# First expert pair's rows: one-hot as weights with x moving in 512 columns, instead of x as weights in 128

## The chip, the cores and the metric

The kernel runs on 1 core of one Trainium2 chip. The metric is device time in microseconds, the median of several runs of the whole program. TensorE works at 2.4 GHz when the granted clock is 1.00, and at 1.2 GHz when it is 0.50.

## The reference, cut to what matters

A block with two layers of mixer and mixture of experts is followed by a second block with attention; 256 tokens, width 1024, float32. The change lies in the expert part of each layer:

```python
g_logits = xt @ w_group            # 4 groups, top 1
e_logits = xt @ w_expert           # 8 experts a group, top 2
...
xi = x_pad[rows]                   # the tokens of one expert
h = jax.nn.silu(xi @ w1[e]) * (xi @ w3[e])
return (h @ w2[e]) * rw[:, None]
```

32 experts with w1 and w3 of 1024x256 and w2 of 256x1024: 3 MB an expert, 96 MB a layer.

## The kernel before, in words

The program is written per engine, with semaphores. A layer runs in this order: norm, mixer (`mix`, whose last steps are the output projection and the router's logits), routing, 16 pairs of experts.

**Weights.** SyncE's queue issues all weights (L583 for w1 and w3, L589 for w2) into a ring of six slots; each load waits until TensorE has freed its slot. During the routing the slots fill up with the first experts' weights.

**Routing.** VectorE picks group and experts for each tile of 128 tokens (`choose`, its last operation L2021 signals `picked`). TensorE counts the picks (L1345, into bank 7). VectorE forms the places (L2033), and from them `first_hot` (L2035), which says for each token whether it stands in a slot of expert 0 or 1; then `token_of`, `slot_of` and `lane_hot_bf` (L2046) for all experts. ScalarE copies the scaled logits out (L1840), which frees banks 4 and 5. TensorE opens the four sum banks with products of zeros (`zero_acc`, L968), and forms tables by slot (`by_slot`, L1354): once the token numbers (bf16), later the gates (fp32). From the token numbers VectorE makes the row numbers (L2074), with which GpSimd fetches the rows of the pairs from 1 on by an indirect DMA from a copy of x in HBM (L826).

**The first pair.** Its rows are not fetched, since they would come late. TensorE forms them with products: for each of the 8 blocks k of the width, and each of the 2 token tiles, x[:, t, block k] is the stationary operand and first_hot the moving one (L1365). The block k takes every eighth element of a row of x. The result, 128 columns for each k, stands turned (width on the partitions) in banks 4 and 6. ScalarE copies it with the gain of each row to `xg` (L1847), four copies a half. Between the halves TensorE forms the token table.

**Pairs.** `expert_pair`: up products (L922, 32 instructions a pair), transposes of the next pair's rows (L862, `gather`), hidden turned (L942), down products (L954), and the sums by token of the pair before (L873). The first pair also forms the gates by slot within its up products. The first slot is freed by the first product of the second half of the up products.

Of the kernel before, what the change touches and what calls it, by code (L numbers as in the profile page):

```python
# [18 lines left out]
ACT = mybir.ActivationFunctionType  # L19
AX = mybir.AxisListType  # L20

P = 128
SEQ = 256
NT = SEQ // P
D = 1024
KD = D // P
# [8 lines left out]
PAIRS = NE // 2  # L35
# [24 lines left out]
HALF = 512  # L60
# [129 lines left out]
def program(nc, io, out, mixer=True, second=True):  # L190
    with ExitStack() as ctx:
# [3 lines left out]
        def sem(name):  # L195
            return ctx.enter_context(nc.semaphore(name))

        bank = [ctx.enter_context(nc.psum_tensor(f"bank{b}", [P, HALF], F32)) for b in range(8)]
        ring = [sb(f"ring{s}", [P, SLOT]) for s in range(RING)]
        x = sb("x", [P, NT, D])  # L200
# [6 lines left out]
        ident, ones = const["ident"], const["ones"]  # L207
# [25 lines left out]
        stats = sb("stats", [P, 16])  # L233
# [24 lines left out]
        expin = nxt(NT, 8)  # L258
        expout = nxt(NT, 8)
# [11 lines left out]
        first_hot = xf[:, :, :, :].rearrange("p t k i -> p (t k i)")[:, 0:NT * P]\  # L271
            .rearrange("p (t e s) -> p t e s", t=NT, e=2)
        lane_hot_bf = nxt(NT * CELL).bitcast(BF16).rearrange("p (t i s) -> p t i s", t=NT, i=2)
        token_of = nxt(NT * NE).bitcast(BF16).rearrange("p (t i e) -> p t i e", t=NT, i=2)
# [8 lines left out]
        x_rows = nxt(2, D)  # L283
# [214 lines left out]
        xfT_ready = sem("xfT_ready")  # L498
        logits_done = sem("logits_done")
        exp_wanted = sem("exp_wanted")  # L500
        kept_or_exp = sem("kept_or_exp")
        picked = sem("picked")

        rows_stored = sem("rows_stored")
        rows_landed = [sem(f"rows_landed{b}") for b in range(2)]
        LAYER_ROWS = [16 * (PAIRS // 2 - 1), 16 * (PAIRS // 2)]
        counted = sem("counted")
        over_ready = sem("over_ready")
        acc_done = sem("acc_done")
        hots_ready = sem("hots_ready")  # L510
# [204 lines left out]
        def _(pool):  # L715
# [33 lines left out]
            for l in range(DEPTH):  # L749
                m = PER * l  # L750
                if mixer:
# [7 lines left out]
                    half = ROPE // 2  # L759
                    for a in range(2):  # L760
                        g1, g2 = [qk_gain[:, a, NOPE + half * i:NOPE + half * (i + 1)].unsqueeze(1)
                                  .broadcast_to([P, NT, half]) for i in range(2)]
                        for i, (trig, g) in enumerate(((0, g1), (1, g2), (1, g1), (0, g2))):
                            ins = pool.tensor_tensor(rope_table(a, i), cos_sin[:, trig, :, :], g, ALU.mult)
# [40 lines left out]
                plan = plans[l]  # L805

                copied(pool, plan, "yTa0", "yTa1")
                pool.memset(x_rows[:, 0, :], 0.0)
                pool.memset(y_words[:, 1, :], 0.0)
                step(pool.memset(onehot_words[:, 1, :], 0.0))  # L810
                copied(pool, plan, "out0", "out1")
# [45 lines left out]
        def _(pe):  # L857
# [107 lines left out]
            def zero_acc():  # L965

                for b in range(4):
                    pe.matmul(bank[b][:, :], zeros[:, 0:P], zeros, start=True, stop=False, skip_group_check=True)  # L968

            for s in range(RING):  # L970

# [363 lines left out]
            for l in range(DEPTH):  # L1335
                turn(l, range(1 if l == 0 else NT))
                mix(l)
                zero_acc()

                pe.wait_ge(picked, 2 * l + 2)  # L1340
                before, every = counts_bf[:, 0, :], counts_bf[:, 1, :]
                for at, parts in ((0, ((before, 0),)), (1, ((before, 1), (every, 0))), (2, ((every, 0), (every, 1)))):
                    terms = [(mask, t, i) for mask, t in parts for i in range(2)]
                    for n, (mask, t, i) in enumerate(terms):
                        ins = pe.matmul(bank[7][:, at * NE:(at + 1) * NE], mask, pick[:, t, i, :],  # L1345
                                        start=(n == 0), stop=(n == len(terms) - 1))
                ins.then_inc(counted, 1)

                def by_slot(dst, hot, values, kinds):

                    for e in range(2):
                        for t in range(NT):
                            for i in range(2):
                                ins = pe.matmul(dst[CELL * e:CELL * (e + 1), 0:kinds * PAIRS], hot[:, t, i, 0:CELL],  # L1354
                                                values(t, i, e),
                                                start=(t == 0 and i == 0), stop=(t == NT - 1 and i == 1))
                    ins.then_inc(tables_made, 1)

                q0 = l * PAIRS
                pe.wait_ge(kept_or_exp, 3 * l + 2)  # L1360
                pe.wait_ge(hots_ready, 2 * l + 1)
                for half in range(2):
                    for k in range(4):
                        for t in range(NT):
                            ins = pe.matmul(bank[4 + 2 * half][:, k * P:(k + 1) * P],  # L1365
                                            x[:, t, :].rearrange("p (i k) -> p k i", k=KD)[:, 4 * half + k, :],
                                            first_hot[:, t, :, :].rearrange("p e s -> p (e s)"),
                                            start=(t == 0), stop=(t == NT - 1))
                    ins.then_inc(main["gathered"], 1)
                    if half == 0:  # L1370
                        pe.wait_ge(hots_ready, 2 * l + 2)
                        by_slot(bank[7][:, P:P + PAIRS], lane_hot_bf,
                                lambda t, i, e: token_of[:, t, i, :].rearrange("p (q e) -> p e q", e=2)[:, e, :], 1)

                def gates_by_slot():

# [243 lines left out]
        def _(act):  # L1620
# [213 lines left out]
            for l in range(DEPTH):  # L1834
                if mixer:
                    norm_turn(l)
                    mix(l)
                for t in range(NT):
                    act.wait_ge(picked, 2 * l + t + 1)
                    act.activation(logits[:, t, :], bank[4 + t][:, 0:N_GROUPS + NE], ACT.Copy,  # L1840
                                   scale=stats[:, 8 + t:9 + t]).then_inc(kept_or_exp, 1)
                act.wait_ge(loaded_ffn, ROUTER_LOADS * (l + 1))
                for half in range(2):
                    act.wait_ge(main["gathered"], 2 * l * PAIRS + half + 1)
                    for i in range(4):
                        k = 4 * half + i
                        ins = act.activation(xg[:, 0, k, :], bank[4 + 2 * half][:, i * P:(i + 1) * P], ACT.Copy,  # L1847
                                             scale=row_gain_in[:, k:k + 1])
                    ins.then_inc(main["xg_ready"], 1)
                act.wait_ge(exp_wanted, l + 1)  # L1850
                act.activation(expout[:, :, 0:7], expin[:, :, 0:7], ACT.Exp).then_inc(kept_or_exp, 1)
                q0 = l * PAIRS
                act.wait_ge(gates_ready, 2 * l + 2)
                last = PAIRS // 2 - 1
                with act.Fori(0, last) as j:
                    for par in range(2):
                        expert_pair(par, 2 * j + (q0 + par), main)
                for par in range(2):
                    expert_pair(par, 2 * last + (q0 + par), main, last=(par == 1))
                act.wait_ge(over_ready, l + 1)  # L1860
                n_over = act.value_load(overint[0:1, l, CELLS_OVER:CELLS_OVER + 1], min_val=0, max_val=2)
                with act.If(n_over > 0):
                    S = extra[l]
                    act.wait_ge(extra_slots[l], OVER_PAIRS + 1)
                    with act.Fori(0, n_over) as j:
                        for par in range(2):
                            expert_pair(par, 2 * j + par, S)
                with act.Else():
                    act.nop()
# [80 lines left out]
        def _(dve):  # L1950
# [74 lines left out]
            def route(l):  # L2025
# [3 lines left out]
                choose(l, 1)  # L2029
                dve.wait_ge(picked, 2 * l + 2)  # L2030
                step(dve.tensor_tensor(first_place, pick[:, :, 0, 0:2], pick[:, :, 1, 0:2], ALU.add))
                dve.wait_ge(counted, l + 1)
                step(dve.scalar_tensor_tensor(first_place, bank[7][:, 0:NT * NE].rearrange("p (t e) -> p t e", t=NT)  # L2033
                                              [:, :, 0:2], 1.0, first_place, ALU.add, ALU.mult))
                dve.tensor_tensor(first_hot, const["iota"][:, 1:CELL + 1].unsqueeze(1).unsqueeze(1)  # L2035
# [10 lines left out]
                dve.tensor_tensor(lane_hot_bf, lanes, places, ALU.is_equal).then_inc(hots_ready, 1)  # L2046
                dve.tensor_tensor(lane_hot[:, :, :, 0:CELL], lanes, places, ALU.is_equal)

                dve.wait_ge(kept_or_exp, 3 * l + 2)
                gl, el = logits[:, :, 0:N_GROUPS], logits[:, :, N_GROUPS:]  # L2050
                gw = [groupwork[:, :, i, :] for i in range(3)]
                rb = lambda n: rowmax[:, :].unsqueeze(2).broadcast_to([P, NT, n])
# [28 lines left out]
            def finish_route(l):  # L2081


                dve.wait_ge(kept_or_exp, 3 * l + 3)
                step(dve.tensor_reduce(expin[:, :, 0:1], expout[:, :, 0:N_GROUPS], AX.X, ALU.add))
                step(dve.tensor_tensor(expin[:, :, 1:2], expout[:, :, 5:6], expout[:, :, 6:7], ALU.add))
                step(dve.tensor_tensor(expin[:, :, 0:1], expin[:, :, 0:1], expin[:, :, 1:2], ALU.mult))
                step(dve.reciprocal(expin[:, :, 0:1], expin[:, :, 0:1]))
                step(dve.tensor_tensor(expin[:, :, 0:1], expin[:, :, 0:1], expout[:, :, 4:5], ALU.mult))
                rstd = stats[:, 8:8 + NT]  # L2090
                step(dve.tensor_tensor(gates.rearrange("p i t -> p t i"), expin[:, :, 0:1].broadcast_to([P, NT, 2]),
                                       expout[:, :, 5:7], ALU.mult))
                step(dve.tensor_tensor(gates, gates, rstd.unsqueeze(1).broadcast_to([P, 2, NT]), ALU.mult))
                by_token = gates.rearrange("p i t -> p t i").unsqueeze(3).broadcast_to([P, NT, 2, NE])
                step(dve.tensor_tensor(gate_of[:, :, :, 0, :], pick, by_token, ALU.mult))
                dve.tensor_tensor(gate_of[:, :, :, 1, :], pick,
                                  rstd.unsqueeze(2).unsqueeze(3).broadcast_to([P, NT, 2, NE]), ALU.mult)\
                   .then_inc(gates_ready, 1)
# [605 lines left out]
```

## Time and profile before

| | us |
|---|---|
| median of 3 runs | 1101.12 |
| lowest, highest | 1099.44, 1103.45 |
| the profiled execution | 1100.17 |
| its span | 1098.3 |
| mean granted clock of TensorE | 0.992 |

A span runs from the first instruction to the last on the core; the time of the execution lies 1.87 us above it. An fp32 product is two matmul instructions, each with its weight load (PEld). "Idle before" a row is the time in which its engine waited, and behind the arrow stands what ended it.

### The profile page before, as it was taken

The numbers are of one execution on the slowest core, as the hardware profiler recorded it, in microseconds if no ns is written. First come the engines' busy times: TensorE is split into PE (matmuls) and PEld (weight loads), VectorE is DVE, ScalarE is ACT, GpSimd is POOL, SyncE is SP. The second block draws the span as 40 slices with busy tenths as digits, with TensorE's granted clock in tenths as the row PEclk, the third lists the DMA queues.
The fourth block names the chain that finished last, engine by engine and source line by source line (L and its number), as shares of the span: only waits on it lengthen the run. The fifth ranks groups of instructions, "written<-read, shape, count | busy, mean of one in ns | idle before, by whom it ended". The sixth has DMA issues, their size and how long they took to land.

```text
span 1098.3 us, 12899 instructions
## 1 busy us (share of the span) xinstructions
PE 1053.3 (96%) x4563; PEld 543.0 (49%) x4597; DVE 401.2 (37%) x975; ACT 272.8 (25%) x530; POOL 99.7 (9%) x146
## 2 busy tenths in 40 slices
PE   6999999999999999999989999999999999999998
PEld 3577655333333334676655333333334844555543
DVE  1164424443443351462343443344430222333221
ACT  4244322111111003334321111111112005564300
POOL 1220221000000002210121000000000200000000
PEclk9899999999999999999999999999999999999999
DMA  8526227999999996427246999999979537822000
GB/s 299 195 78 256 103 87 246 386 412 411 412 413 412 411 399 208 128 82 302 77 172 228 398 412 413 412 412 412 413 289 389 199 36 201 310 85 77 1 1 38
DMA packets 95326, 280.44 MB, mean 255 GB/s; under 512 B 15957, under 2 KB 29699, under 8 KB 86960
## 3 DMA queue, kind: packets, MB, share of 16 engines
q1 hardware_dynamic: 90208, 273.27, 65.9%
q0 software_dynamic: 5072, 6.56, 1.7%
q8 instruction: 29, 0.48, 0.2%
q14 instruction: 17, 0.14, 0.0%
HBM read 286.98 MB, written 4.72 MB: 266 GB/s over the span
## 4 chain that ended last, share of the span: by engine, by line
PE 75%; SPq 14%; DMA 5%; issue 2%; ACT 2%; DVE 1%; ACTq 0%; DVEq 0%
PE bank L1464 12%; PE bank L922 12%; SPq L583 11%; PE bank L1029 8%; PE bank L954 6%; PE bank L1226 5%; PE bank L1043 5%; PE bank L873 4%; DMA ring<-in_w 3%; SPq L589 3%; PE bank L1610 3%; PE bank L1594 3%; PE bank L1482 3%; PE bank L862 2%; DMA ring<-in_w_in 2%
## 5 line engine op out<-in xcount | busy, mean ns | idle before, releaser
L922 PE MATMUL bank<-ring,arena 128*64 128x512 f32 x1024 | 229.2, 596 | 4.4 <-DMA ring<-in_w 4.4
L1464 PE MATMUL bank<-ring,xfT 128*128 128x512 f32 x320 | 141.5, 596 | 0.0
L922 PEld LDWEIGHTS bank<-ring,arena 128*64 128x64 f32 x1024 | 70.9, 137 | 136.5 <-issue 126.3
L954 PE MATMUL bank<-ring,arena 128*64 128x512 f32 x512 | 116.9, 598 | 0.0
L1029 PE MATMUL bank<-ring,xfT 128*128 128x384 f32 (+2 forms) x256 | 100.1, 544 | 4.8 <-DMA ring<-in_w_in 4.8
L1464 PEld LDWEIGHTS bank<-ring,xfT 128*128 128x128 f32 x320 | 59.3, 190 | 69.3 <-issue 68.3
L873 PE MATMUL bank<-arena 128*128 128x512 bf16 x352 | 86.4, 379 | 1.9 <-issue 0.3
L1632 ACT ACTIVATE arena<-bank 128x512 bf16<-128x512 f32 (+1 forms) x64 | 38.2, 597 | 190.1 <-PE bank L954 190.1
L1969 DVE TENSOR_TENSOR arena<-bank,arena 128x512 f32<-128x512 f32 x60 | 41.5, 691 | 119.4 <-ACT arena L1632 119.4
L1029 PEld LDWEIGHTS bank<-ring,xfT 128*128 128x128 f32 x256 | 49.3, 198 | 45.6 <-issue 26.2
L954 PEld LDWEIGHTS bank<-ring,arena 128*64 128x64 f32 x512 | 33.9, 136 | 68.4 <-issue 68.4
L1625 ACT ACTIVATE arena<-bank,arena 128x256 f32<-128x256 f32 x32 | 15.1, 473 | 202.2 <-PE bank L922 202.2
L826 POOL DMA_INDIRECT arena<-x_store,arena x30 | 30.6, 1021 | 378.8 <-PE bank L862 357.9
L1226 PE MATMUL bank<-ring,xfT 128*128 128x512 f32 x128 | 57.4, 596 | 1.2 <-ACT xfT L1782 1.2
L1990 DVE SCALAR_TENSOR_TENSOR arena<-arena,bank 128x256 f32<-128x256 f32 x32 | 15.4, 480 | 116.1 <-ACT arena L1625 116.1
L1043 PE MATMUL bank<-xfT,ring 128*96 128x256 f32 x256 | 56.7, 380 | 0.0
L862 PEld LDWEIGHTS bank<-consts,arena 128*128 128x128 f32 x240 | 31.2, 195 | 48.7 <-issue 48.7
L873 PEld LDWEIGHTS bank<-arena 128*128 128x128 bf16 x384 | 37.7, 98 | 32.6 <-issue 1.6
L1043 PEld LDWEIGHTS bank<-xfT,ring 128*96 128x96 f32 x256 | 41.4, 163 | 13.5 <-issue 0.3
L862 PE MATMUL bank<-consts,arena 128*128 128x128 f32 x240 | 42.6, 300 | 0.0
L1981 DVE TENSOR_TENSOR arena<-bank,row_gain 128x512 f32<-128x512 f32 x60 | 41.2, 687 | 3.5
L1975 DVE TENSOR_TENSOR arena<-arena 128x512 bf16<-128x512 f32 x60 | 38.5, 682 | 0.0
(379 smaller groups left out, 1132.0 us busy)
## 6 DMA issues: line engine op xcount, KB each, us to landing
ring<-in_w SPq DMA_DIRECT2D x256, 512.0 KB
ring<-in_w SPq DMA_DIRECT2D x64, 1024.0 KB
ring<-in_w_in SPq DMA_DIRECT2D x14, 2048.0 KB
ring<-in_w_in SPq DMA_DIRECT2D x8, 1536.0 KB
ring<-in_w_out SPq DMA_DIRECT2D x6, 2048.0 KB
x_store<-x POOLq DMA_DIRECT2D x4, 512.0 KB, 6.2
ring<-in_w_up_moba SPq DMA_DIRECT2D x1, 2048.0 KB
ring<-in_w_up_sb SPq DMA_DIRECT2D x1, 2048.0 KB
```

Source lines behind the costliest of these rows:

```text
L583: sp.dma_start(up_view(s)[:, i, w].rearrange("p k f -> p (k f)"), src)\
L862: ins = pe.transpose(dst[:, i * P:(i + 1) * P], x_rows[:, buf, :].rearrange("p (i k) -> p k i", k=KD)[:, k, :], ident)
L873: ins = pe.matmul(bank[2 * t + n][:, :], onehotT[:, par, t * P:(t + 1) * P], y_parts[:, par, i, n, :], start=False, stop=False, skip_group ...
L922: ins = pe.matmul(bank[5][CELL * e:CELL * (e + 1), :], xg[:, par, 4 * h + k, at:at + CELL], view[:, e, :, k, :], start=(h == 0 and k == 0) ...
L954: ins = pe.matmul(bank[5 + n][CELL * e:CELL * (e + 1), :], turned[:, par, c, CELL * e:CELL * (e + 1)], down_view(s)[:, e, c, n * HALF:(n + ...
L1029: ins = pe.matmul(dst[:, 0:w], xfT[:, k, t * P:(t + 1) * P], unit_view(u, w)[:, k, :], start=(k == 0), stop=(k == KD - 1))
L1043: ins = pe.matmul(dst[hd, h * SEQ:(h + 1) * SEQ], unit_view(u, M_WIDTH)[:, k, (2 * i + h) * M_DIM:(2 * i + h + 1) * M_DIM], xfT[:, k, :], ...
L1226: ins = pe.matmul(bank[plan[name][0]][:, :], xfT[:, k, t * P:(t + 1) * P], unit_view(n, HALF)[:, k, :], start=(first and k == ks[0]), stop ...
L1464: ins = pe.matmul(dst[:, :], xfT[:, k, t * P:(t + 1) * P], w[:, k, :], start=(k == 0), stop=(k == KD - 1))
L1969: dve.tensor_tensor(y_rest[:, n, :], bank[5 + n][:, :], y_parts[:, par, 0, n, :], ALU.subtract)\
L1975: dve.tensor_tensor(y_parts[:, par, 2, n, :], y_rest[:, n, :], y_parts[:, par, 1, n, :], ALU.subtract).then_inc(S["low_ready"], 1)
L1981: dve.tensor_tensor(xg[:, par, 4 * half:4 * half + 4, :], src[:, :].rearrange("p (k s) -> p k s", k=4), row_gain_in[:, 4 * half:4 * half + ...
```

## The change

- The first pair's products have `first_hot` as stationary operand, and x with its width permuted as moving operand, 512 columns at once: four products, two for each half. The result has the slots on the partitions, and goes to banks 4 and 6.
- ScalarE copies each half to `x_rows[:, 0, :]` (two new copies, 128x512). TensorE transposes it back into the same bank, four transposes a half. ScalarE's gain copies to `xg` are as before.
- The token table comes after both halves' products, and before the transposes.
- `add_zeros` accumulates products of zeros (bf16, 512 columns) on the four sum banks: four before the wait for `picked`, two before the wait for `first_hot`.
- GpSimd no longer sets `x_rows[:, 0, :]` to zero.
- The semaphores `kept_or_exp` and `counted` are named `route_acts` and `route_products` and count the new steps too.

```diff
+            def add_zeros(n):
+
+                for i in range(n):
+                    pe.matmul(bank[i % 4][:, :], zeros[:, 0:P], zeros, start=False, stop=False, skip_group_check=True)
...
-                pool.memset(x_rows[:, 0, :], 0.0)
...
                 zero_acc()
 
+                add_zeros(4)
                 pe.wait_ge(picked, 2 * l + 2)
...
-                ins.then_inc(counted, 1)
+                ins.then_inc(route_products, 1)
...
+                add_zeros(2)
                 q0 = l * PAIRS
-                pe.wait_ge(kept_or_exp, 3 * l + 2)
+                pe.wait_ge(route_acts, 5 * l + 2)
                 pe.wait_ge(hots_ready, 2 * l + 1)
                 for half in range(2):
+                    for t in range(NT):
+                        ins = pe.matmul(bank[4 + 2 * half][:, :], first_hot[:, t, :, :].rearrange("p e s -> p (e s)"),
+                                        x[:, t, :].rearrange("p (i k) -> p k i", k=KD)[:, 4 * half:4 * half + 4, :],
+                                        start=(t == 0), stop=(t == NT - 1))
+                    ins.then_inc(route_products, 1)
+                pe.wait_ge(hots_ready, 2 * l + 2)
+                by_slot(bank[7][:, P:P + PAIRS], lane_hot_bf,
+                        lambda t, i, e: token_of[:, t, i, :].rearrange("p (q e) -> p e q", e=2)[:, e, :], 1)
+                for half in range(2):
+                    pe.wait_ge(route_acts, 5 * l + 3 + half)
                     for k in range(4):
-                        for t in range(NT):
-                            ins = pe.matmul(bank[4 + 2 * half][:, k * P:(k + 1) * P],
-                                            x[:, t, :].rearrange("p (i k) -> p k i", k=KD)[:, 4 * half + k, :],
-                                            first_hot[:, t, :, :].rearrange("p e s -> p (e s)"),
-                                            start=(t == 0), stop=(t == NT - 1))
+                        ins = pe.transpose(bank[4 + 2 * half][:, k * P:(k + 1) * P],
+                                           x_rows[:, 0, (4 * half + k) * P:(4 * half + k + 1) * P], ident)
                     ins.then_inc(main["gathered"], 1)
-                    if half == 0:
-                        pe.wait_ge(hots_ready, 2 * l + 2)
-                        by_slot(bank[7][:, P:P + PAIRS], lane_hot_bf,
-                                lambda t, i, e: token_of[:, t, i, :].rearrange("p (q e) -> p e q", e=2)[:, e, :], 1)
...
                 act.wait_ge(loaded_ffn, ROUTER_LOADS * (l + 1))
+                for half in range(2):
+                    act.wait_ge(route_products, 3 * l + 2 + half)
+                    act.activation(x_rows[:, 0, half * HALF:(half + 1) * HALF], bank[4 + 2 * half][:, :], ACT.Copy)\
+                       .then_inc(route_acts, 1)
                 for half in range(2):
                     act.wait_ge(main["gathered"], 2 * l * PAIRS + half + 1)
```

## Rows read from the trace of the kernel before

**Rows 1.** The page: the chain that ended last, shares of the span by engine.

```profile
PE 75%; SPq 14%; DMA 5%; issue 2%; ACT 2%; DVE 1%; ACTq 0%; DVEq 0%
```

**Rows 2.** Stretches: length, busy time of each engine, PEclk, DMA share, GB/s.

```profile
174.30:184.00 9.70, 9.70 (x58) 6.15 (x59) 3.89 (x21) 2.00 (x8) 2.18 (x2) 1.00 0.25 68
...
316.00:405.00 89.00, 86.94 (x408) 33.44 (x410) 40.38 (x92) 12.57 (x20) 4.04 (x4) 1.00 1.02 412
```

**Rows 3.** Chain that ended last, 165 to 195 us, then the weight queue's timeline.

```profile
169.74 4.08 PE bank L1365 x16
173.82 0.24 PE bank L1354 x8
174.05 4.03 PE bank L1365 x16
...
182.72 5.44 SPq L583 DMA_DIRECT2D ring<-in_w  x8
```

**Rows 4.** Timeline: first L922 of layer 0; first products and first L922 of layer 1.

```profile
178.01 5.37 PE L922 MATMUL bank<-ring,arena 128*64 128x512 f32 x24
...
573.80 4.17 PE L1365 MATMUL bank<-xf,x 128*128 128x128 f32 x16 [0.88 <-DVE xf L2035]
...
582.24 5.37 PE L922 MATMUL bank<-ring,arena 128*64 128x512 f32 x24
```

**Rows 5.** Group by shape, 164 to 185 us; then timeline of L1319's loads.

```profile
L1365 PEld LDWEIGHTS bank<-xf,x 128*128 128x128 f32 x32 | 7.8, 335 | 1.0 <-ACT arena L1840 1.0
...
164.03 1.95 PEld L1319 LDWEIGHTS bank<-w_router,xf 128*128 128x128 f32 x16
```

**Rows 6.** Stretches around the routing of layer 0 and of layer 1.

```profile
170.70:171.70 1.00, 1.00 (x6) 1.00 (x6) 0.96 (x4) 0.00 (x0) 0.00 (x0) 0.50 1.00 418
...
174.70:175.70 1.00, 1.00 (x6) 1.00 (x6) 0.83 (x6) 0.35 (x2) 0.31 (x1) 1.00 0.12 49
...
578.00:579.00 1.00, 1.00 (x11) 0.97 (x12) 0.54 (x4) 0.93 (x4) 0.00 (x0) 0.50 0.10 25
```

**Rows 7.** Chain: contiguous 512-column products; timeline: four transposes, contiguous (L1308), stepped (L862).

```profile
147.26 10.30 PE bank L1226 x24
...
162.64 0.60 PE L1308 MATMUL bank<-consts,x 128*128 128x128 f32 x4
...
185.75 0.71 PE L862 MATMUL bank<-consts,arena 128*128 128x128 f32 x4
```

**Rows 8.** Groups by shape, whole span: loads of transposes; ScalarE copies, one in its timeline.

```profile
L862 PEld LDWEIGHTS bank<-consts,arena 128*128 128x128 f32 x240 | 31.2, 195 | 48.7 <-issue 48.7
...
L1308 PEld LDWEIGHTS bank<-consts,x 128*128 128x128 f32 x32 | 3.7, 141 | 3.4 <-issue 2.1 <-DVE x L2439 1.3
...
L1817 ACT ACTIVATE xf<-bank 128x512 f32<-128x512 f32 x8 | 4.5, 593 | 24.1 <-PE bank L1308 24.1
...
173.91 1.14 ACT L1847 ACTIVATE arena<-bank,row_gain 128x128 f32<-128x128 f32 x4 [5.21 <-PE bank L1365]
```

**Rows 9.** Timeline of layer 0: three products of zeros, then the wait for the picks.

```profile
166.15 0.81 PE L968 MATMUL bank<-consts 128*128 128x512 bf16 x3
...
168.44 0.41 PE L1345 MATMUL bank<-arena 128*128 128x32 bf16 x10 [1.48 <-DVE arena L2021]
```

**Rows 10.** Timeline of layer 0: slot masks, fetch, gates; last, landing times of line L826.

```profile
170.69 0.42 DVE L2046 TENSOR_TENSOR arena<-consts,arena 128x256 bf16<-128x256 f32 x1
...
175.39 1.17 POOL L826 DMA_INDIRECT arena<-x_store,arena  x1 [8.37 <-DMA x_store<-x]
...
179.40 0.16 DVE L2085 TENSOR_REDUCE arena<-arena 128x2 f32<-128x8 f32 x1 [2.63 <-ACT arena L1851]
...
181.11 0.29 DVE L2096 TENSOR_TENSOR arena<-arena,stats 128x128 f32<-128x128 bf16 x1
...
182.78 0.14 PEld L1354 LDWEIGHTS bank<-arena 128*64 128x64 f32 x1 [0.29 <-issue]
...
DMA to landing us min/median/max: 3.2/7.1/8.5
```

More of the change, by code:

```diff
@@ L500, in program @@
         exp_wanted = sem("exp_wanted")
-        kept_or_exp = sem("kept_or_exp")
+        route_acts = sem("route_acts")
         picked = sem("picked")
@@ L506, in program @@
         LAYER_ROWS = [16 * (PAIRS // 2 - 1), 16 * (PAIRS // 2)]
-        counted = sem("counted")
+        route_products = sem("route_products")
         over_ready = sem("over_ready")
@@ L1840, in _ @@
                     act.activation(logits[:, t, :], bank[4 + t][:, 0:N_GROUPS + NE], ACT.Copy,
-                                   scale=stats[:, 8 + t:9 + t]).then_inc(kept_or_exp, 1)
+                                   scale=stats[:, 8 + t:9 + t]).then_inc(route_acts, 1)
                 act.wait_ge(loaded_ffn, ROUTER_LOADS * (l + 1))
+                for half in range(2):
+                    act.wait_ge(route_products, 3 * l + 2 + half)
+                    act.activation(x_rows[:, 0, half * HALF:(half + 1) * HALF], bank[4 + 2 * half][:, :], ACT.Copy)\
+                       .then_inc(route_acts, 1)
                 for half in range(2):
@@ L1850, in _ @@
                 act.wait_ge(exp_wanted, l + 1)
-                act.activation(expout[:, :, 0:7], expin[:, :, 0:7], ACT.Exp).then_inc(kept_or_exp, 1)
+                act.activation(expout[:, :, 0:7], expin[:, :, 0:7], ACT.Exp).then_inc(route_acts, 1)
                 q0 = l * PAIRS
@@ L2031, in route @@
                 step(dve.tensor_tensor(first_place, pick[:, :, 0, 0:2], pick[:, :, 1, 0:2], ALU.add))
-                dve.wait_ge(counted, l + 1)
+                dve.wait_ge(route_products, 3 * l + 1)
                 step(dve.scalar_tensor_tensor(first_place, bank[7][:, 0:NT * NE].rearrange("p (t e) -> p t e", t=NT)
@@ L2047, in route @@
                 dve.tensor_tensor(lane_hot[:, :, :, 0:CELL], lanes, places, ALU.is_equal)
-                dve.wait_ge(kept_or_exp, 3 * l + 2)
+                dve.wait_ge(route_acts, 5 * l + 2)
                 gl, el = logits[:, :, 0:N_GROUPS], logits[:, :, N_GROUPS:]
@@ L2081, in finish_route @@
             def finish_route(l):
-                dve.wait_ge(kept_or_exp, 3 * l + 3)
+                dve.wait_ge(route_acts, 5 * l + 5)
                 step(dve.tensor_reduce(expin[:, :, 0:1], expout[:, :, 0:N_GROUPS], AX.X, ALU.add))
```

## The prediction

> **What bounds the kernel now.** Read the page first. The chain that ended last is TensorE for 75% of the span, and for 19% the queue that issues the weights and their transfers [rows 1]. So the stages have to be told apart. The table of stretches does it: from 316 to 405 us (the second half of the experts of layer 0) the DMA engines are saturated at 412 GB/s, and TensorE follows them. Between 174.3 and 184 us, just before, the engines are nearly empty at 68 GB/s: the ring of six weight slots is full, and nothing can be loaded until TensorE frees a slot [rows 2]. What frees it is the expert products themselves: the weight queue issues its next block at 182.72, when the second half of the first pair's up products (L922) has begun [rows 3]. So the experts of a layer end at (first slot freed) + (bytes left at 412 GB/s), and a microsecond won or lost ahead of the first L922 is won or lost at the end of the layer. Nothing is absorbed on the way, since the stream has been standing still.
>
> What leads up to the first L922 is read from the chain in order of time: small VectorE operations up to L2035 (the one-hot of the first places), which the first product has waited for, then TensorE without a gap: eight products of 128 columns (16 instructions, L1365), the small table sums (L1354), eight more products, and L922 [rows 3, 4]. ScalarE copies each half out with a gain as it is done. From the first L1365 to the first L922 layer 0 takes 178.01 - 169.74 = 8.27 us, layer 1 takes 582.24 - 573.80 = 8.44 us [rows 3, 4]. These 16.7 us are what the change works on.
>
> **Why the old products are slow.** Each of them is a weight load of x and a run of 128 columns. 32 loads take 7.8 us, 0.244 us each; 16 ordinary fp32 loads of 128 columns, at L1319, take 1.95 us, 0.122 us each [rows 5]. The granted clock was 0.50 within layer 0's first half and 1.00 in its second, and both took the same 4.1 us [rows 3, 6]. So the loads set the pace, not the array, and the difference from L1319 is that x is read with a step of 8 elements (32 bytes).
>
> **Part by part, for one layer.** Time runs from the first product.
>
> 1. *The products.* Removed: 16 products (32 instructions), 4.08 + 4.03 = 8.1 us [rows 3]. Added: 4 products of 512 columns, first_hot contiguous as weights, x with step 8 as moving data: 8 instructions. A contiguous 512-column fp32 instruction comes every 10.30 / 24 = 0.429 us [rows 7]; 8 x 0.429 = 3.43 us. This is the lower bound. No row shows moving data with that step. The upper bound is the strided load: 0.252 us for 128 columns (4.03 / 16, [rows 3]) gives 1.01 us for 512, so 8 x 1.01 = 8.06 us. The evidence is split. The same tile with the same step speaks for the upper bound. For the lower one: the transposes of L862 load x_rows with the very same step, 195 ns instead of the 141 ns of the contiguous L1308, but four of them still take only 0.71 us against 0.60 to 0.66 us [rows 7, 8]; 128 strided elements are then read in at most 0.71 / 4 = 0.18 us. And a matmul consumes its moving columns at 0.84 ns each, so it needs no faster reads than that. I take the lower bound, and hold it only a little likelier than the other.
>
> 2. *The table sums* (L1354) now come behind both halves: 0.24 us in the chain [rows 3]. lane_hot_bf, which they wait for, is done at 171.1, before the 173.2 at which they are now wanted [rows 10]. They then end at 3.7 us instead of 4.3 us: the row numbers and the gates are 0.6 us earlier.
>
> 3. *ScalarE's two new copies*, 128x512 from a bank: 0.59 us each [rows 8]. The first lies under the second half's products. The second starts at about 3.43 + 0.16 + 0.09 and ends at 4.27 us.
>
> 4. *The transposes of the first half* start after the table sums at 3.67: a first load of 0.14 us and 0.60 us for four [rows 7], to 4.41 us. Queued ahead of the gain copies on ScalarE is the second new copy, which is done at 4.27: a margin of only 0.14 us. The second half's transposes follow under ScalarE's work.
>
> 5. *The gain copies* of the first half: 0.09 us to wake and 1.14 us [rows 8], then 0.05 us for TensorE: L922 at 5.69 us. The second half is ready 1.2 us later and is wanted only 3.5 us after L922 has begun, so it costs nothing.
>
> 6. *Zero products.* Three like them take 0.81 us from the first start to the last end [rows 9]; I count 0.22 us for each, since they overlap, and 0.27 us would change nothing. Four stand in the wait for the picks, where TensorE is idle for 1.48 us, and two in the wait for first_hot, idle for 0.88 us [rows 4, 9]: 0.9 of 1.48 and 0.45 of 0.88 us, so they delay nothing. What they are worth is the clock. It stood at 0.50, 1.2 GHz, at 170.7, after these two waits, and in layer 1 still at 578 [rows 6]. The old products didn't mind; new ones at full rate would.
>
> 7. *The memset of x_rows* (GpSimd) goes. GpSimd waits behind it in any case, 8.37 us for the store of x alone [rows 10]. No gain and no loss.
>
> The sum: 3.43 + 0.24 + 0.74 + 0.09 + 1.14 + 0.05 = 5.69 us against 8.27 and 8.44: 2.6 and 2.7 us won, 5.3 us together. Against the profiled execution's 1100.17 us this is 1094.9; the median of the runs is 0.95 above that execution, and I give 1095.8 us.
>
> **What could be late next.** The gates: the second set of L1354 stands behind 24 instructions of L922. It was issued at 182.8, while the last gate operation, L2096, ended at 181.4 [rows 10]. After the change it is wanted 2.6 us earlier, at 180.2. ScalarE's Exp (L1851) stands behind the second gain copies, which end at 169.74 + 5.69 + 1.14 = 176.6; its inputs, ready at 179.40 - 2.63 = 176.8 before, are ready by 176.2. The thread behind it (L2085 to L2096) takes 2.0 us, with the Exp about 2.3: gates at 178.9, no stall. The fetch of pair 1's rows was issued at 175.39, held by the store of x, not by the tables [rows 10]; its like land in 3.2 to 8.5 us, and its transposes come at 183.2 instead of 185.75 [rows 7]. In layer 0 the weights' queue is empty then, so I take a landing near the short end.
>
> **Rivals.**
>
> *Strided moving data reads as slowly as strided weights (the other side).* 8.06 + 2.26 = 10.32 us a layer: 2.05 and 1.9 us lost, 3.9 together, 1105.0 us. It decides from 0.75 us an instruction, where 8 of them use up the 6.0 us that the other steps leave. For it: the load row of this very tile. Against it: L862.
> The Trainium skill, Advanced Engine Details and Errata, SBUF Cachelines, speaks for this rival: SBUF lines have 16 bytes, and reads that hit each line only once pay a penalty. By that rule every moving column here pays, since 32 bytes lie between two of them. The trace agrees for the loads of L1365 (0.244 against 0.122 us a load) and only weakly for L862 (195 against 141 ns).
> A worse form of it reads the strided data twice, once for each half of the fp32 product: 16.1 us, 10 us lost a layer, 1121 us.
>
> *The clock stays low all the same.* The zero products don't keep it up, or the fall comes at another place. Full-rate products then take 0.85 us for each instruction that starts at half clock, up to 3.4 us more a layer; with half to all of it, the gain of 2.6 becomes between 0.9 won and 0.8 lost. About 1101 us. For it: the clock fell in both layers. Against it: TensorE is busy for 1.3 us more of that stretch than before.
>
> *The stream doesn't start earlier*: the start of the experts moves, but something else holds the weights. Then no change, 1101 us. The near-empty engines in [rows 2] speak against it.
>
> **Chances.** Forecast 0.48. Slow moving reads 0.30, their worse form 0.07. Clock 0.09. Hidden 0.06. The predicted time is the forecast's, 1095.8. The forecast's own range is 1094 to 1098. The range reaches to the slow reads at 1105.0 with 0.8 on top: 1094 to 1105.8. It leaves out the worse form and little else. A difference of 0.3%, 3.3 us, is about what can be told from no change. Faster: the forecast less a few misses, 0.47. Same: clock and hidden, and some of the slow reads, which lie right at the bound (3.9 against 3.3 us): 0.24. Slower: 0.29.
>
> **What the profile after would show.** Eight products with 512 columns on the new line, 0.43 us apart (forecast), 1.0 (rival) or 1.9 (worse form). First L922 5.7 us after the first of them. The granted clock 1.00 from the picks to L922. Two ScalarE copies of 0.59 us. The weights at over 400 GB/s 2.6 us earlier, and the end of each layer's experts moved by just as much. The prediction is wrong if the products are slower than 0.75 us an instruction, or if the end of the experts doesn't follow their start.

## The result: 0.25% slower

| | median of 20 runs, us |
|---|---|
| before | 1100.06 |
| after | 1102.90 |

The ratio is 1.0025, with a 95% interval from 1.0013 to 1.0036: about 2.8 us slower. Faster by 5.3 us was forecast. What came is the first rival, strided moving reads, with a somewhat smaller price than its 3.9 us.

The chain that ended last of the changed kernel, layer 0, answers to [rows 3]:

```profile
168.99 0.43 DVE xf L2048
169.42 0.14 issue
169.56 7.57 PE bank L1370 x8
177.12 0.24 PE bank L1359 x8
177.36 0.60 PE bank L1380 x4
177.96 0.02 issue
177.98 1.15 ACT arena L1860 x4
179.13 0.14 issue
179.27 5.37 PE bank L921 x24
```

The eight product instructions (L1370) alone take 7.57 us, nearly the 8.1 us of the 32 that they replace. Then come the table sums, the transposes (L1380) and the gain copies (L1860), 2.14 us in all. The old form had only the table sums (0.24 us) beside its products, and L922 followed them at once. The up products, now L921, start 179.27 - 169.56 = 9.71 us after the first product. Before, it was 8.27. The timeline of the changed kernel shows the same 9.71 us in layer 1, where it was 8.44 ([rows 4]):

```profile
575.62 7.57 PE L1370 MATMUL bank<-x,xf 128*128 128x512 f32 x8 [0.44 <-DVE xf L2048]
...
585.33 5.37 PE L921 MATMUL bank<-ring,arena 128*64 128x512 f32 x24 [0.80 <-ACT arena L1860]
```

1.44 + 1.27 = 2.7 us lost, against 2.8 measured. The group by shape, and the stretches of the changed kernel (length, TensorE, loads, VectorE, ScalarE, GpSimd, granted clock, DMA share, GB/s):

```profile
L1370 PE MATMUL bank<-x,xf 128*128 128x512 f32 x16 | 15.1, 1103 | 0.9 <-DVE xf L2048 0.9
```

```profile
169.50:171.50 2.00, 1.94 (x3) 0.57 (x4) 1.82 (x8) 0.00 (x0) 0.00 (x0) 1.00 1.00 416
171.50:173.50 2.00, 2.00 (x4) 0.56 (x3) 0.10 (x1) 0.00 (x0) 0.00 (x0) 1.00 1.04 436
...
175.50:177.00 1.50, 1.50 (x2) 0.00 (x0) 0.00 (x0) 0.00 (x0) 0.00 (x0) 1.00 0.00 0
```

One instruction lasts 1103 ns, and (7.57 - 1.10) / 7 = 0.92 us lie between two starts, while a contiguous one came every 0.43 us [rows 7]. The granted clock is 1.00 all the while, where [rows 6] had 0.50. Nor is it the weights' stream: at 175.5 the DMA engines are silent, and the pace is the same.

The profiled execution spans 1104.4 us, 6.1 more than that of before. Of these, 2.7 are the ones above. The rest is spread over stretches that are the same in both programs. From the start of the last row of up products of layer 1 to the end of the span alone (813.70 us after, 810.10 before) it is 290.7 us against 288.2. Single executions of one kernel differ by that much (1099.69 to 1107.79 us for the changed one); the medians do not rest on it.

### The profile page after: what moved, and what is told of

Same layout as the page of the kernel before. It is cut to its first block, busy times and chain, and to the rows that moved or that the text cites. A ratio compares the mean times of both kernels' runs of the same rounds, so it can differ in the third digit from the quotient of the medians.

```text
span 1104.4 us, 12861 instructions
## 1 busy us (share of the span) xinstructions
PE 1059.2 (96%) x4543; PEld 534.9 (48%) x4577; DVE 399.6 (36%) x975; ACT 275.2 (25%) x534; POOL 97.6 (9%) x144
## 4 chain that ended last, share of the span: by engine, by line
PE 75%; SPq 15%; DMA 5%; issue 2%; ACT 2%; DVE 1%; ACTq 0%; DVEq 0%
PE bank L1473 12%; PE bank L921 12%; SPq L583 11%; PE bank L1033 8%; PE bank L953 6%; PE bank L1230 5%; PE bank L1047 5%; PE bank L872 4%; DMA ring<-in_w 3%; SPq L589 3%; PE bank L1603 3%; PE bank L1619 3%; PE bank L1491 3%; PE bank L861 2%; DMA ring<-in_w_in 1%
## 5 line engine op out<-in xcount | busy, mean ns | idle before, releaser
L921 PE MATMUL bank<-ring,arena 128*64 128x512 f32 x1024 | 229.4, 596 | 7.2 <-DMA ring<-in_w 5.6
L921 PEld LDWEIGHTS bank<-ring,arena 128*64 128x64 f32 x1024 | 71.5, 137 | 139.3 <-issue 129.2
L825 POOL DMA_INDIRECT arena<-x_store,arena x30 | 30.6, 1021 | 383.1 <-PE bank L861 358.4
```

The lines of the kernel that those rows point to most:

```text
L921: ins = pe.matmul(bank[5][CELL * e:CELL * (e + 1), :], xg[:, par, 4 * h + k, at:at + CELL], view[:, e, :, k, :], start=(h == 0 and k == 0) ...
```

## The experiments

Ratios are to the kernel before, from runs on the same chip; E1 to E4, E5 to E8 and E9 to E11 ran on three different chips. "First to up" is the time from the first product to the first up product, read from the timeline of each, layer 0 and layer 1.

**E1, x in runs of four.** The same products and bytes, in the order i, k instead of k, i, so that four adjacent elements (16 bytes) are read of every 32 bytes.

```diff
-                                        x[:, t, :].rearrange("p (i k) -> p k i", k=KD)[:, 4 * half:4 * half + 4, :],
+                                        x[:, t, :].rearrange("p (i k) -> p i k", k=KD)[:, :, 4 * half:4 * half + 4],
...
-                                           x_rows[:, 0, (4 * half + k) * P:(4 * half + k + 1) * P], ident)
+                                           x_rows[:, 0, half * HALF:(half + 1) * HALF]
+                                           .rearrange("p (i k) -> p k i", k=4)[:, k, :], ident)
```

> The changed kernel, with x moved in runs of four adjacent elements (16 bytes) out of every 32: the same four products and bytes, only the order of the 512 columns differs, and the transposes pick every fourth element of x_rows instead. Theory A (the cost is that each moving column lies in a 16-byte line of its own): a product instruction takes 0.43 us instead of 0.92, first L922-like product 5.8 us after the first of them instead of 9.7, 3.9 us a layer less than the changed kernel; about 5 us less than the kernel before in all, ratio 0.995. Theory B (any moving operand with two dimensions or with gaps is slow): 0.92 us and the changed kernel's ratio, 1.0025. Theory C (the size of 512 fp32 columns with first_hot as weights is slow for another reason): 0.92 us too.

Measured: 1096.43 us against 1100.41; ratio 0.9956 (0.9939 to 0.9973). Its chain:

```profile
169.44 3.67 PE bank L1370 x8
173.11 0.24 PE bank L1359 x8
173.35 0.69 PE bank L1380 x4
174.04 0.02 issue
174.07 1.15 ACT arena L1861 x4
175.22 0.14 issue
175.35 5.36 PE bank L921 x24
```

3.67 us for the products instead of 7.57, and everything behind them as in the changed kernel but for 0.09 us in the transposes, whose loads now have a step of four. First to up: 5.91 us in both layers. That is as expected of theory A, and theories B and C fall: the operand still has two dimensions and gaps, and 512 columns with first_hot as weights run at full speed.

**E2, x whole.** The moving operand is `x[:, t, half * HALF:(half + 1) * HALF]`. The transposes pick every eighth element of the whole row, and so wait for both copies.

```diff
-                    pe.wait_ge(route_acts, 5 * l + 3 + half)
+                    if half == 0:
+                        pe.wait_ge(route_acts, 5 * l + 4)
```

> The changed kernel, with x moved in 512 adjacent elements; the rows then stand in their natural order, so that the transposes of the first half must wait for both copies and load every eighth element, as L862 does. Theory A: 0.43 us an instruction; up products some 6.4 us after the first product (0.6 to 0.7 us later than with runs of four, for the wait on the second copy), 4 us less than before in all, ratio 0.9965. Theory B: 0.43 us as well; it differs from theory A only together with the run of runs of four. Theory C: 0.92 us, 1.003.

Measured: 1094.73 us; ratio 0.9952 (0.9934 to 0.9969). Its timeline:

```profile
167.99 3.67 PE L1370 MATMUL bank<-x,xf 128*128 128x512 f32 x8 [0.44 <-DVE xf L2050]
174.38 5.37 PE L921 MATMUL bank<-ring,arena 128*64 128x512 f32 x24 [0.88 <-ACT arena L1862]
```

The products take 3.67 us, exactly as with runs of four, so a run of 16 bytes costs as little as one without an end. First to up is 6.39 us, 0.48 later than E1 for the wait on the second copy. The whole time doesn't tell these two apart; their intervals overlap.

**E5, E6, E7, other steps.** The moving operand takes every second, fourth or sixteenth element. The width of the first pair's rows is then in a wrong order. One run each, for the duration of a product; their whole times (1095.64, 1101.41 and 1105.11 us, against 1100.38 before) are single values and carry no weight.

```diff
-x[:, t, :].rearrange("p (i k) -> p k i", k=KD)[:, 4 * half:4 * half + 4, :]
+x[:, t, :].rearrange("p (i k) -> p k i", k=2)[:, half, :]                        # E5
+x[:, t, :].rearrange("p (i k) -> p k i", k=4)[:, 2 * half:2 * half + 2, :]       # E6
+x[:, t, :].rearrange("p (i k) -> p k i", k=16)[:, 8 * half:8 * half + 8, :]      # E7
```

> The changed kernel with x moved at a step of 2 elements (8 bytes), so that the width of the first pair's rows is in a wrong order and its values are not the reference's. Looked at: the time of one 512-column product instruction. If a 16-byte line that is hit twice is free: 0.43 us. If any step beyond one element costs: 0.92 us. If the cost is per line: 0.46 us.

> The same at a step of 4 elements (16 bytes), each line hit once; the first pair's width is in a wrong order. If the price is for each new line: 0.92 us as at step 8. If it grows with the distance in bytes: between 0.43 and 0.92.

> The same at a step of 16 elements (64 bytes); the first pair's width is in a wrong order. If the price is for each new line: 0.92 us. If it grows with the distance: well above 0.92.

The groups by shape of E5, of E6 and of E7 (mean ns of one behind the comma):

```profile
L1370 PE MATMUL bank<-x,xf 128*128 128x512 f32 x16 | 7.7, 620 | 0.9 <-DVE xf L2048 0.9
```

```profile
L1370 PE MATMUL bank<-x,xf 128*128 128x512 f32 x16 | 14.8, 1084 | 0.9 <-DVE xf L2048 0.9
```

```profile
L1370 PE MATMUL bank<-x,xf 128*128 128x512 f32 x16 | 14.2, 1040 | 0.9 <-DVE xf L2048 0.9
```

| step in elements (bytes) | eight products, us | start to start, us |
|---|---|---|
| 1, or runs of four (E2, E1) | 3.67 | 0.44 |
| 2 (8), E5 | 3.83 | 0.46 |
| 4 (16), E6 | 7.42 | 0.91 |
| 8 (32), the change | 7.57 | 0.92 |
| 16 (64), E7 | 7.08 | 0.86 |

The last column is (eight products - one) / 7. The price stands between 8 and 16 bytes and doesn't grow beyond: it goes by how many new 16 bytes are read, not by the distance. All three runs are as expected of a price per line. At 0.92 / 512 = 1.8 ns for each new 16 bytes, the 256 of E5 take 0.46 us, as measured, and the 128 of E1 and E2 take 0.23 us, which vanishes under the 0.43 us that the 512 columns need. So the larger of the two counts, not their sum. That a 16-byte line has fixed bounds is not shown: no run reads four elements across one.

**E8, stepped loads alone.** The kernel before, x as weights in adjacent elements. The first pair's width is in a wrong order.

```diff
-                                            x[:, t, :].rearrange("p (i k) -> p k i", k=KD)[:, 4 * half + k, :],
+                                            x[:, t, (4 * half + k) * P:(4 * half + k + 1) * P],
```

> The kernel before with its stationary x read as 128 adjacent elements instead of every eighth; the first pair's width is in a wrong order. It prices the stepped load by itself. Expected: a load at 0.12 us instead of 0.244, a half 2.0 to 2.1 us instead of 4.1; at the lower clock a product of 128 columns takes 0.21 us, so that a half that falls into it takes up to 3.5 us. Up products 4.3 to 6 us after the first product instead of 8.3; some 5 to 8 us less in all, ratio 0.993 to 0.9955, if a gain ahead of the experts reaches the end.

Measured: 1096.29 us against 1100.38; ratio 0.9961 (0.9943 to 0.9978). Its timeline:

```profile
168.27 3.75 PE L1365 MATMUL bank<-xf,x 128*128 128x128 f32 x16 [0.88 <-DVE xf L2035]
172.28 3.00 PE L1365 MATMUL bank<-xf,x 128*128 128x128 f32 x16
175.22 5.37 PE L922 MATMUL bank<-ring,arena 128*64 128x512 f32 x24
```

6.95 us to the up products, where 4.3 to 6 were expected, and 4.3 us less in all, where 5 to 8 were: most of what the step had cost has turned into the other cost, the clock. It was 0.50 from before the first product to 174.3 us of this trace, and the 16 instructions of the first half then take 3.75 us, 0.23 each, though they read without a step. At the clock of 1.00 the same 16 take 2.02 us (E9, below). The stepped loads had hidden the low clock.

**E10, zero products alone.** The kernel before, with `add_zeros(4)` and `add_zeros(2)` at the change's places.

> The kernel before and nothing but the six products of zeros of the change. The granted clock is 1.00 during the first products, in both layers. If these are paced by their stepped loads: no change, ratio 1.000, each half still 4.1 us. If the clock paces them in part: up to 1 us a layer less, 0.998.

Measured: 1099.71 us against 1099.81; ratio 1.0001 (0.9988 to 1.0014). The stretches of this kernel:

```profile
168.00:170.00 2.00, 1.56 (x7) 1.51 (x7) 1.86 (x7) 0.00 (x0) 0.00 (x0) 1.00 1.01 422
170.00:172.00 2.00, 2.00 (x10) 2.00 (x9) 0.54 (x3) 0.00 (x0) 0.00 (x0) 1.00 1.02 428
```

Its chain:

```profile
168.52 4.04 PE bank L1372 x16
172.56 0.24 PE bank L1360 x8
172.80 4.03 PE bank L1372 x16
```

The clock stays at 1.00 where [rows 6] had 0.50, in layer 1 too, and the halves take 4.04 and 4.03 us, nearly as before. First to up is 8.24 and 8.23 us, 0.03 and 0.21 less. The zeros do their work, and it is worth almost nothing while stepped reads set the pace.

**E3 and E4, no zeros.** E1 and the changed kernel without `add_zeros(4)` and `add_zeros(2)`.

> Runs of four, without the six products of zeros in each layer. If they keep the clock up: the granted clock is 0.50 during the products in at least one layer, an instruction then takes 0.85 us, and 1.7 to 3.4 us a layer are lost against runs of four, which brings it back to the kernel before (ratio 1.000). If they do nothing: same time as runs of four, 0.995.

> The changed kernel without the six products of zeros. If the strided reads set the pace of the products, the clock may fall to 0.50 and the products stay at about 0.92 us an instruction, since 0.85 us for the array at 1.2 GHz is hidden under that: the changed kernel's time, ratio 1.0025. If the array sets the pace, it is slower by 1.7 us or more.

E3: 1098.66 us; ratio 0.9987 (0.9974 to 0.9999). E4: 1103.34 us; ratio 1.0032 (1.0019 to 1.0046). E3's timeline and stretches:

```profile
169.40 5.19 PE L1368 MATMUL bank<-x,xf 128*128 128x512 f32 x8 [0.88 <-DVE xf L2047]
...
573.63 6.17 PE L1368 MATMUL bank<-x,xf 128*128 128x512 f32 x8 [0.88 <-DVE xf L2047]
```

```profile
169.00:171.00 2.00, 1.60 (x2) 0.83 (x3) 1.86 (x7) 0.00 (x0) 0.00 (x0) 0.51 0.99 416
...
575.00:577.00 2.00, 2.00 (x3) 0.67 (x2) 0.64 (x4) 0.00 (x0) 0.00 (x0) 0.50 1.02 430
```

E4's timeline and a stretch:

```profile
167.68 7.68 PE L1368 MATMUL bank<-x,xf 128*128 128x512 f32 x8 [0.88 <-DVE xf L2046]
```

```profile
169.00:171.00 2.00, 2.00 (x3) 0.67 (x3) 0.69 (x4) 0.00 (x0) 0.00 (x0) 0.50 1.04 434
```

Without zeros both fall to 1.2 GHz. In E3 the products grow from 3.67 to 5.19 and 6.17 us. In E4 they take 7.68 instead of 7.57. So the zeros are worth 1.5 us in layer 0 and 2.5 in layer 1 with runs of four, and nothing that can be measured in the whole time of the change as it was made.

**E11, a delay of known length.** 24 products of zeros between the first pair's last product and its up products, in the kernel before.

```diff
+                for i in range(24):
+                    pe.matmul(bank[i % 4][:, :], zeros[:, 0:P], zeros, start=False, stop=False, skip_group_check=True)
```

> The kernel before with 24 products of zeros (24 x 0.216 = 5.2 us) in each layer between the first pair's last product and its up products. If time ahead of the first up product reaches the end undiminished: 10.4 us more, ratio 1.0094. If the stream of the weights absorbs some: less, down to 1.000.

```profile
178.03 5.34 PE L1376 MATMUL bank<-consts 128*128 128x512 bf16 x24
183.30 5.37 PE L922 MATMUL bank<-ring,arena 128*64 128x512 f32 x24
```

The up products start 183.30 - 178.03 = 5.27 us late, and as much in layer 1. The time is 1111.32 us against 1099.81, the ratio 1.0096 (1.0074 to 1.0118), 10.6 us (8.1 to 13.0) for 2 x 5.27 = 10.5. Nothing is absorbed that these runs could tell.

**E9, x sorted ahead.** The kernel before with both sets of zeros, its 32 small products, and x as weights without a step, from two copies that ScalarE makes in its waits for the picks.

```diff
+        apart = [x_rows[:, 0, :].rearrange("p (k i) -> p k i", k=KD), xg[:, 1, :, :]]
...
-                                            x[:, t, :].rearrange("p (i k) -> p k i", k=KD)[:, 4 * half + k, :],
+                                            apart[t][:, 4 * half + k, :],
...
+                    act.activation(apart[t], x[:, t, :].rearrange("p (i k) -> p k i", k=KD), ACT.Copy)\
+                       .then_inc(x_apart, 1)
                     act.wait_ge(picked, 2 * l + t + 1)
```

> The kernel before and the six products of zeros, with its 32 products as they were, but x as weights read without a step: ScalarE has copied x, its width sorted by k, into x_rows and the unused half of xg while it waits for the picks (two copies of 1024 columns, 1.1 us each, in its gaps of 1.1 and 2.1 us). If the stepped read is the whole price: a load takes 0.12 us, a half 2.0 us at the full clock, up products 4.3 us after the first product against 8.3 before and 5.9 with runs of four: 4 us a layer, 8 us in all, ratio 0.9927. If 128-column products cost more than their loads: less; the half of 16 instructions would stay at 3 us or more and the ratio at 0.996.

Measured: 1091.90 us against 1099.81; ratio 0.9931 (0.9916 to 0.9946). Its timeline:

```profile
165.52 2.06 ACT L1848 ACTIVATE arena<-x 128x1024 f32<-128x1024 f32 x1
...
167.65 2.07 ACT L1848 ACTIVATE arena<-x 128x1024 f32<-128x1024 f32 x1
...
170.40 2.02 PE L1374 MATMUL bank<-xf,arena 128*128 128x128 f32 x16 [0.44 <-DVE xf L2046]
172.59 2.05 PE L1374 MATMUL bank<-xf,arena 128*128 128x128 f32 x16
174.57 5.37 PE L923 MATMUL bank<-ring,arena 128*64 128x512 f32 x24
```

A half takes 2.02 us, and the up products start 4.17 us after the first. This is the best of the runs, 7.6 us under the kernel before by the ratio. ScalarE's copies were mis-sized in the expectation: 2.06 us each, not 1.1. They fit in all the same: the second ends at 169.72, and first_hot is the last thing waited for.

The runs on one line each (all but the single ones, E5 to E7), with the difference read from the timelines set beside the one measured:

| | first to up, layer 0 / 1, us | both against before's 8.27 + 8.44 | measured ratio - 1, as us of 1100 |
|---|---|---|---|
| change | 9.71 / 9.71 | +2.7 | +2.8 |
| E1 | 5.91 / 5.91 | -4.9 | -4.8 |
| E2 | 6.39 / 6.39 | -3.9 | -5.3 |
| E3 | 7.44 / 8.41 | -0.9 | -1.4 |
| E4 | 9.82 / 9.81 | +2.9 | +3.5 |
| E8 | 6.95 / 6.90 | -2.9 | -4.3 |
| E9 | 4.17 / 4.17 | -8.4 | -7.6 |
| E10 | 8.24 / 8.23 | -0.2 | +0.1 |
| E11 | 13.46 / 13.45 | +10.2 | +10.6 |

Each measured value has an interval of 1.2 to 2.5 us to either side (4 to 20 executions), and every value of the third column lies in it.

## Why the prediction was wrong

- **The step that failed is part 1, the products, where the lower bound was chosen.** It put 8 x 0.43 = 3.43 us; they took 7.57. The upper bound, 8.06, was 6% too high. The row of the same tile with the same step was the right one to go by. E1, E2 and the sweep of steps show that the way x is read is the cause, since the products differ in nothing else. The measured 1102.9 us lies in the stated range only because that range took in this rival; the forecast's own, 1094 to 1098, doesn't reach it.
- **The argument for the lower bound.** "A matmul consumes its moving columns at 0.84 ns each, so it needs no faster reads than that" has the right number and draws the wrong end from it. 0.84 ns is what the reads would have to keep up with. With a new 16 bytes for every column they give one in 1.8 ns. L862's transposes were no evidence. Why their loads stand a step of 32 bytes better than those of L1365 no run here tells. They don't follow the sweep either: such a load takes 141 ns adjacent (L1308), 196 at 8 bytes (L942), 210 at 16 (E1, whose four transposes were 0.09 us slower) and 195 at 32 (L862).
- **The rule on lines** (the Trainium skill, Advanced Engine Details and Errata, SBUF Cachelines: 16-byte lines, two hits on one absorb the latency) was cited for the rival. The sweep agrees with it for moving reads: 8 bytes 0.46 us, 16 bytes 0.91.
- **Parts 2 to 5** hold in their durations. Forecast 2.26 us from the products' end to L922, measured 179.27 - 177.13 = 2.14. With products at full rate (E1) the whole way is 5.91 us against the 5.69 forecast, and the time 1096.4 against the 1095.8 forecast.
- **Part 6** was right: the zeros delay nothing, and keep the clock at 1.00 (E10), so the rival of the low clock falls. That they are worth nothing here follows from part 1 (E4).
- **Part 7** and the gates: the change shows no new wait in the up products. The second L1359 starts 5.17 us behind the first L921, where it was 5.20 before. But part 2's "0.6 us earlier" for the row numbers fell with part 1. In layer 0 the table sums end at 177.36 us instead of 174.05, and the fetch of pair 1's rows (L825) is issued at 178.60 instead of 175.39 ([rows 10]). Its rows came in time all the same: their transposes start 7.71 us behind the first L921, against 7.74 before. In the change the fetch has 8.4 us for it, where it had 10.4.
- **What bounds the kernel** was right and is now shown: a delay of 5.27 us a layer ahead of the up products costs 10.6 us in all (E11), and gains come through as well, within the intervals of the table. The weight queue issues its next block 4.68 us behind the first L921 (at 183.95), as it did 4.71 us behind the first L922 ([rows 3]). The rival in which the stream hides it falls. So does the worse form of the first rival, 1.9 us an instruction.

## What to carry to other kernels

Look at the step of the innermost dimension of each fp32 operand before counting TensorE's columns. Here a step of 16 bytes or more doubled the time of the moving read, and a step of 32 bytes that of a product's load (0.244 us against 0.126 in E9). Reading four adjacent elements and skipping four was free, so it is often enough to swap the order of two dimensions and let the next step undo it. A slow read hides a low clock and a low clock hides a slow read. Take one away, and the other has to be taken away with it to see the gain. And where a stage is fed by a stream that stands still until the stage starts, expect each microsecond ahead of its start to count in full.

## What was not expected of the hardware

- ScalarE seems to pay for the step too: a copy of 1024 fp32 columns of x with a step of 32 bytes takes 2.06 us (E9). Its squares of the same tile, read without a step, take 1.06 us in the same trace. The function differs as well, and no run changes the step alone:

```profile
159.67 1.06 ACT L1832 ACTIVATE arena<-x 128x1024 f32<-128x1024 f32 x1
```

- A step of 64 bytes is slightly cheaper than one of 16 or 32: 7.08 us against 7.42 and 7.57 for eight products.
- At the granted clock of 0.50 stepped products lose only 0.1 us in 7.6 (E4). The clock is 0.50 there until about 173 us, past the first five instructions, and their loads start 0.92 us apart (168.74, 169.66, 170.58, 171.50, 172.42), as in the change at 1.00. The pace of these reads doesn't follow TensorE's clock.
